# A fused two-block transformer kernel: residual and norms of the first stage by rows, modulation weights loaded in feature order, pooling branch inside the last attention steps

## The reference

```python
mod = silu(c) @ w_ada + b_ada                     # 6 x 1024
shift1, scale1, gate1, shift2, scale2, gate2 = split(mod, 6)
h = rmsnorm(x, norm_mix_g) * (1 + scale1) + shift1
proj = h @ w_in                                   # 512 pool, 3 x 512 qkv, 2 x 1024 gates
attn = attention(rope(q), rope(k), v)             # 8 heads of 64, causal
pooled = pool_mixer(proj[:, :512])                # causal window means, mixed by groups
merged = sigmoid(g_pool) * (pooled @ w_branch_pool) + sigmoid(g_attn) * (attn @ w_branch_attn)
x = x + gate1 * (merged @ w_out)
h2 = rmsnorm(x, norm_ffn_g) * (1 + scale2) + shift2
x = x + gate2 * peer_ffn(h2)                      # 8 heads x top 16 of 16384 experts per token
x = rmsnorm(x, norm_final_g)
```

## Time and profile before

| | us |
|---|---|
| median of 3 runs | 1271.32 |
| lowest, highest | 1270.78, 1272.63 |
| profiled execution | 1268.42 |
| its span, first to last instruction | 1266.6 |
| TensorE, VectorE, ScalarE busy | 1081.7, 844.0, 434.0 |
| mean granted TensorE clock | 0.947 |

### The profile page before, as it was taken

The page is one execution under the profiler, slowest core; times in us unless marked ns, Lnnn a source line. Parts: engine busy times, 40 slices in busy tenths (PEclk is TensorE's granted clock), DMA queues, the critical chain, the costliest instruction groups (busy, mean ns, idle before and its releaser), DMA issues.

```text
span 1266.6 us, 13601 instructions
## 1 busy us (share of the span) xinstructions
PE 1081.7 (85%) x5030; PEld 738.0 (58%) x5030; DVE 844.0 (67%) x1887; ACT 434.0 (34%) x879; POOL 290.7 (23%) x260
## 2 busy tenths in 40 slices
PE   1698998879899878886768778777899998999997
PEld 1697888745455334332324333322498767999986
DVE  5986774477768887878885555554664455887853
ACT  2543362232122232221322111111455444666542
POOL 0000000044344544354545435444000000000000
PEclk9798998889999989799889989899999989999999
DMA  9966643399999999999999999999773403455440
GB/s 385 404 249 266 247 185 133 133 382 398 421 396 422 421 422 421 419 413 421 421 421 421 422 421 422 421 422 421 322 291 133 150 28 122 167 200 200 177 156 33
DMA packets 47154, 389.89 MB, mean 308 GB/s; under 512 B 5361, under 2 KB 5617, under 8 KB 7154
## 3 DMA queue, kind: packets, MB, share of 16 engines
q0 software_dynamic: 36864, 268.45, 51.2%
q1 hardware_dynamic: 10226, 120.59, 24.6%
HBM read 387.97 MB, written 1.05 MB: 307 GB/s over the span
## 4 chain that ended last, share of the span: by engine, by line
PE 51%; DMA 27%; DVE 14%; ACT 4%; POOL 2%; issue 2%; SPq 0%; DVEq 0%; POOLq 0%
DMA ring<-in_uv,idx 25%; PE ps L1349 18%; PE ps L1605 14%; PE ps L1729 5%; PE ps L1371 3%; DVE ring L1153 3%; PE ps L1401 2%; POOL ring L457 2%; DVE ring_r L806 2%; PE ps L1660 2%; PE ps L1493 2%; PE ps L1511 2%; DMA ring<-in_w_ada 2%; DVE ring L817 1%; ACT ring_r L473 1%
## 5 line engine op out<-in xcount | busy, mean ns | idle before, releaser
L1605 PE MATMUL ps<-ring,probT 128*128 128x512 f32 x1024 | 493.9, 631 | 115.6 <-ACT probT L673 115.6
L1153 DVE CUSTOM_DVE_ANT_0 ring<-h2t,ring 128x1024 f32<-128x1024 f32 x256 | 309.7, 1225 | 176.0 <-DMA ring<-in_uv,idx 175.5
L457 POOL DMA_INDIRECT ring<-in_uv,idx x256 | 290.5, 1135 | 594.5 <-PE ps L1605 289.4
L1605 PEld LDWEIGHTS ps<-ring,probT 128*128 128x128 f32 x1024 | 200.7, 201 | 368.5 <-issue 209.8
L1349 PE MATMUL ps<-util_r,ring_r 128*128 128x256 f32 x1312 | 218.1, 284 | 0.4 <-DVE util_r L1125 0.4
L806 DVE TENSOR_TENSOR ring_r<-ring,ring_r 128x1024 fp32r<-128x1024 f32 x142 | 167.5, 1220 | 44.7 <-ACT ring_r L473 44.7
L1349 PEld LDWEIGHTS ps<-util_r,ring_r 128*128 128x128 f32 x1312 | 182.6, 190 | 4.7 <-issue 3.9
L473 ACT ACTIVATE ring_r<-ring 128x1024 fp32r<-128x1024 f32 x142 | 142.2, 1049 | 47.2 <-DMA ring<-in_w_in 23.7
L668 ACT ACTIVATE prob<-prob 128x4 f32<-128x4 f32 (+2 forms) x74 | 15.2, 205 | 370.4 <-DVE prob L1153 370.3
L1349 PE MATMUL ps<-h_r,ring_r 128*128 128x256 f32 x704 | 125.2, 281 | 0.6 <-DVE util_r L1125 0.6
L673 ACT ACTIVATE probT<-ct,prob 128x128 f32<-128x128 f32 x256 | 82.9, 391 | 74.9 <-DVE prob L1159 72.3
(11 more groups left out here) (210 smaller groups left out, 1005.4 us busy)
## 6 DMA issues: line engine op xcount, KB each, us to landing
ring<-in_w_in SPq DMA_DIRECT2D x13, 2048.0 KB, 10.6
ring<-in_w_ada SPq DMA_DIRECT2D x11, 2048.0 KB, 13.7
ring<-in_w_up SPq DMA_DIRECT2D x11, 2048.0 KB, 7.8
ring<-in_w_down SPq DMA_DIRECT2D x6, 2048.0 KB, 7.9
ring<-in_w_out SPq DMA_DIRECT2D x4, 2048.0 KB, 9.1
ring<-in_w_q SPq DMA_DIRECT2D x3, 2048.0 KB, 7.6
ring<-in_w_br SPq DMA_DIRECT2D x2, 2048.0 KB, 8.0
ring<-in_uv,idx POOLq DMA_INDIRECT x256, 17.5
```

Of the source, the lines that this page charges most:

```text
L457: e.indirect_dma_start(out=row_buf[n], out_offset=None, in_=uv, in_offset=bass.IndirectOffsetOnAxis(ap=idx[:, tt, k:k + 1], axis=0)).then_inc(
L1153: e.tensor_tensor_reduce(u, h2t[:, tt, :], u, 1.0, 0.0, ALU.mult, ALU.add, av[:, tt, n % 128:n % 128 + 1]).then_inc(*made.put(("dot", n)))
L1605: ins = e.matmul(acc[half][:, :], diag[:, n % 8, :], row_buf[n][:, D + half * 512:D + (half + 1) * 512], start=(k == 0), stop=(k == 127))
```

## The change

- x is loaded by rows (token on the partition). The first norm takes squares with a sum on ScalarE, a root, a reciprocal and a diagonal matrix of it on VectorE; eight products of each 128 tokens with that diagonal turn and scale x. The same again for the second norm, after an output projection by rows (512 columns a matmul, high parts of four pieces at a time) and a residual by rows with gate1 spread over the partitions. `residual_rows` is gone.
- The chunks of w_ada come in the order 0, 2, ("in", 0), 1, 3, so that shift and scale of features 0 to 511 are there first; the products with ("in", 0) are made for these features, then for the others. c comes as one row and is spread by TensorE. The constants come in two transfers.
- VectorE's list: four more low pieces stand earlier; the copies of the values go to ScalarE. Pieces 22 to 25 stand ahead of ("ada", 8).
- The four branch quarters of the pooling input are made in attention steps 7 to 10; their pieces, gatings and sigmoids in steps 5 to 10. Chunk 11 of w_ada is multiplied in step 4.

The core of the diff:

```diff
-    first = ([("ada", i) for i in range(4)] + [("in", 0)]
+    first = ([("ada", 0), ("ada", 2), ("in", 0), ("ada", 1), ("ada", 3)]
...
-    slots = [0, 1, 2, 3, 4, 0, 1, 2, 3, 1, 4, 3, 0, 2, 0, 1, 0, 3, 0, 2, 0, 2, 1, 3, 0, 2, 1, 3, 5] + [1, 0, 2, 3] * 6 + [1]
+    slots = [0, 1, 4, 2, 3, 0, 1, 2, 3, 1, 4, 3, 0, 2, 0, 1, 0, 3, 0, 2, 0, 2, 1, 3, 0, 2, 1, 3, 5] + [1, 0, 2, 3] * 6 + [1]
...
-            e.dma_start(ct[:, :], consts).then_inc(*once["ct"].put(0))
+            e.dma_start(csig[0:1, :], c_in).then_inc(*once["c"].put(0))
+            e.dma_start(ct[:, 0:CONST_FIRST], consts[:, 0:CONST_FIRST]).then_inc(*once["ct"].put(0))
             e.dma_start(cl[:, :], cols).then_inc(*once["cl"].put(0))
-            e.dma_start(crow, c_in.broadcast_to([P, D])).then_inc(*once["c"].put(0))
-            load(0)
-            load(1)
-            e.dma_start(x_sb[:, :, :].rearrange("p k t -> p (k t)"), xT).then_inc(*once["x"].put(0))
-            for n in (2, 3, 4):
+            e.dma_start(x_sb[:, :, :].rearrange("p k t -> p (k t)"), x_in).then_inc(*once["x"].put(0))
+            for n in range(5):
                 load(n)
+            e.dma_start(ct[:, CONST_FIRST:], consts[:, CONST_FIRST:]).then_inc(*once["ct2"].put(0))
...
+            act.wait_ge(once["ct"], 0)
+            sqrt_table(43)
+            for tt in range(2):
+                act.wait_ge(once["x"], 0)
+                e.activation(squared[tt], xt[:, tt, :], ACT.Square, accum_out=col(1, tt, "squares")).then_inc(
+                    *acted.put(("row squares", 1, tt, 1)))
+            for tt in range(2):
+                row_root(1, tt)
+            def modulated(k):
+                act.wait_ge(done, ("turned rows", 1, k // 2))
+                act.wait_ge(made, ("aff1", k // 4))
+                e.activation(h_sb[:, k, :], pair(("turned rows", k // 2))[:, k % 2, :], ACT.Identity,
+                             bias=mod[:, k:k + 1], scale=aff[:, k:k + 1]).then_inc(*acted.put(("modulated", k)))
+                act.wait_ge(acted, ("modulated", k))
+                e.activation(hi_r[:, k, :], h_sb[:, k, :], ACT.Copy).then_inc(*acted.put(("x high", 1, k)))
+            split_high(0)
+            modulated(0)
+            split_high(1)
+            for k in range(1, 4):
+                modulated(k)
+            split_high(2, 3)
+            for k in range(4, 8):
+                modulated(k)
             split_high(*range(4, 10))
...
+            for tt in range(2):
+                act.wait_ge(done, ("tokens", 3, tt))
+                e.activation(vt[:, tt, :], bank(("tokens", 3, tt))[:, :], ACT.Copy).then_inc(*acted.put(("v", 3, tt)))
...
+            sqrt_table(44)
+            for half in range(2):
...
+                e.activation(gate1[:, HALF[half]], bank(("gate1", half))[:, :], ACT.Copy).then_inc(
+                    *acted.put(("gate1", half)))
             for z in range(4):
                 act.wait_ge(made, ("merge", z))
                 act.wait_ge(done, ("pv", 1, 7))
                 e.activation(xm_hi[:, 2 * z:2 * z + 2, :], merged[:, 2 * z:2 * z + 2, :], ACT.Copy).then_inc(
                     *acted.put(("xm high", z)))
-            split_high(*range(44, 48))
-
-            squares(2, h_sb, made, lambda k: ("x1", k))
-            root(2, "eps")
-            shifted(2, h_sb, mod[:, 24:32])
+                split_high(44 + z)
+            def shifted(tt, k):
+                act.wait_ge(done, ("turned x1", tt, k // 4))
+                act.wait_ge(made, "aff2")
+                c = k % 4 * P
+                e.activation(h_sb[:, k, tile[tt]], bank(("turned x1", tt, k // 4))[:, c:c + P], ACT.Identity,
+                             bias=mod[:, 24 + k:25 + k], scale=aff[:, 8 + k:9 + k]).then_inc(
+                    *acted.put(("shifted", tt, k)))
+            row_squares(2, 0)
+            row_root(2, 0)
+            for k in range(KD):
+                shifted(0, k)
+            row_squares(2, 1)
+            row_root(2, 1)
+            for k in range(4):
+                shifted(1, k)
...
+            for tt in range(2):
+                row_diagonal(1, tt)
...
+            ada(0)
+            ada(2)
+            affine1(0)
+            split_low(0, 1)
+            for k in range(4):
+                x_low(1, h_sb, hi_r, k)
+            split_low(2, 3)
+            ada(1)
             ada(3)
-            split_low(0, 1)
...
-            for k in range(KD + 2):
-                if k < KD:
-                    e.tensor_scalar(h_sb[:, k, :], h_sb[:, k, :], aff[:, k:k + 1], mod[:, k:k + 1], ALU.mult,
-                                    ALU.add).then_inc(*made.put(("scaled", 1, k)))
-                if k >= 2:
-                    x_low(1, h_sb, hi_r, k - 2)
-
-            split_low(*range(2, 6))
+            affine1(1)
+            for k in range(4, 8):
+                x_low(1, h_sb, hi_r, k)
+            split_low(*range(4, 8))
             ada(4)
-            split_low(*range(6, 10))
+            split_low(*range(8, 12))
             ada(5)
-            split_low(*range(10, 14))
+            split_low(12, 13)
             rope("q")
-            split_low(14, 15)
+            split_low(*range(14, 18))
             ada(6)
-            split_low(16, 17)
+            split_low(18, 19)
             rope("k")
-            split_low(18, 19)
+            split_low(20, 21)
             ada(7)
-            split_low(*range(20, 24))
-            for tt in range(2):
-                dve.wait_ge(done, ("tokens", 3, tt))
-                e.tensor_copy(vt[:, tt, :], bank(("tokens", 3, tt))[:, :]).then_inc(*made.put(("v", 3, tt)))
+            split_low(*range(22, 26))
             ada(8)
...
+                if i == 6:
+                    four_low("xp", pT, A3r[:, 5])
+                split_low(*beside_br.get(i, ()))
+                if i >= 8:
+                    pool_gated(i - 8)
             four_low("xy", yT, A3r[:, 4])
...
+            pool_gated(3)
+            split_low(43)
...
                 dve.wait_ge(acted, ("xm high", z))
                 e.tensor_tensor(lo_r[:, 2 * z:2 * z + 2, :], m, xm_hi[:, 2 * z:2 * z + 2, :].bitcast(F32),
                                 ALU.subtract).then_inc(*made.put(("xm low", z)))
...
-
-            reciprocal(2)
-            for k in range(KD):
-                scaled(2, h_sb, x_sb, k, aff[:, 8:16])
+                if z > 0:
+                    split_low(43 + z)
+            split_low(47)
+            for tt in range(2):
+                rows_added(2, tt)
+                row_part(2, tt)
+                row_diagonal(2, tt)
+            for k in range(4, KD):
+                dve.wait_ge(done, ("turned x1", 1, 1))
+                e.tensor_scalar(h_sb[:, k, tile[1]], bank(("turned x1", 1, 1))[:, (k - 4) * P:(k - 3) * P],
+                                aff[:, 8 + k:9 + k], mod[:, 24 + k:25 + k], ALU.mult, ALU.add).then_inc(
+                    *made.put(("shifted", k)))
...
+            mixer = [group(("tokens", 0, tt)) for tt in range(2)]
+            for k0 in (0, 4):
+                for z in (0, 2):
...
+                    wait_low(q + 1)
+                    for tt in range(2):
+                        o = mixer[tt][:, z * P:(z + 2) * P].rearrange("p (q n) -> p q n", q=2)
+                        for k in range(k0, k0 + 4):
+                            pe.wait_ge(made, ("x low", 1, k))
+                            for n, (w, x3) in enumerate(((wh, hi_r), (wh, lo_r), (wl, hi_r))):
+                                ins = e.matmul(o, x3[:, k, tile[tt]], w[:, k, :, :], start=(z == 0 and k == 0 and n == 0),
+                                               stop=(z == 2 and k == 7 and n == 2))
+                        if z == 2 and k0 == 4:
+                            ins.then_inc(*done.put(("tokens", 0, tt)))
...
+                if i >= 7:
+                    branch(0, i - 7)
+            for z in range(4):
+                branch(1, z)
+                if z == 0:
+                    for half in range(2):
+                        o = group(("gate1", half))
+                        pe.wait_ge(made, "mod2")
...
+            for tt in range(2):
+                for half in range(2):
+                    o = group(("mix1", tt, half))[:, :]
+                    o4 = o.rearrange("p (q n) -> p q n", q=4)
...
+                    wait_low(QUARTER["out", half, 3])
+                    for k in range(KD):
+                        pe.wait_ge(made, ("xm low", k // 2))
+                        for n, (to, w, x3) in enumerate(((o4, wh, xm_hi), (o4, wh, lo_r), (o, wl, xm_hi))):
+                            ins = e.matmul(to, x3[:, k, tile[tt]], w[:, k], start=(k == 0 and n == 0),
+                                           stop=(k == KD - 1 and n == 2))
+                    ins.then_inc(*done.put(("mix1", tt, half)))
+                    banks.give(("mix1", tt, half), made, ("gated rows", 2, tt, half))
+            for tt in range(2):
+                turned_x1(tt)
```

429 lines of the change are left out of this document (207 added, 222 removed).

## The result

The changed kernel takes 1277.24 us, median of 8 runs (1274.10 to 1280.83), beside 1271.68 for the kernel before in the same comparison (8 runs). The ratio is 1.0043, with a 95% interval of 1.0028 to 1.0058: slower by 0.43%. The forecast was 1271.0 with a range up to 1276.0, so both the forecast and its range were missed. Its profiled execution took 1275.14, with a span of 1273.3; the one before took 1268.42, with 1266.6.

What follows compares the result with a forecast made beforehand. DMA-bound gathers (262 to 899 us) stay fixed, so only the first query matmul shifts: output projection 224.0 plus norm 6.8 gives 230.8 against 231.2, -0.4, hence 1271 us; range 1265.5 to 1276.

Steps and rivals of the forecast that it cites:

- VectorE's stand for ("in", 6): Before the attention: ("in", 6), queued behind chunk 8, lands 13.1 after its pair's issue; VectorE's lead of 5 is gone.
- Start, chunk 7, VectorE's stand: Up to the first mask: first projections done 49.2, chunk 7 done 94.4, VectorE stands from 97, first mask 115.5.
- Second wait to head 4: TensorE waits about 128 to 131; ScalarE's probabilities copy ends 140.7, then 2.2 to head 4's scores at 142.9.
- Steps 7 to 10: Four pooling-branch quarters between attention head steps, 2.9 each; TensorE ends these at 183.8.
- Attention branch: Four quarters after a wait of some 3 for the attention's low parts; with gate1, 1.7, they end at 200.1.
- Merge: VectorE's merge steps with a piece each, 3.9, follow the branch quarters; last low piece ready at 206.9.
- The norm: Output projection to queries: 6.8, including second squares 1.4, root, reciprocal and diagonal 0.9, four small matmuls 0.9, shift 0.4.
- Rival (d): Merge and norm by rows slower, by handovers or 512-column matmuls: +3, 1274.3; chance 0.08.
- (a): Transfers without a tail: both pairs land 11.7 after issue, chain 2.8 shorter, 1268.2; chance 0.20.
- (b): VectorE does not stand at ("in", 6); attention begins 5 to 9 earlier, 7 reaches the end, 1264.3; chance 0.13.
- (c): Lower clock behind TensorE's waits at 110 and 128, counted as nothing in the forecast: +4.5, 1275.8; chance 0.17.
- The late arrival is made up here: Output projection ends at 224.0 against 224.3, as half of its work starts before the merge ends.

Runs made afterwards that it cites:

- run 1: Changed kernel with chunk 8 multiplied on VectorE ahead of low pieces 24 and 25, not behind them: 1267.01 us, ratio to the kernel before 0.9968.
- run 2: Changed kernel with SyncE issuing ("in", 6) ahead of chunk 8 and ("in", 7) ahead of chunk 9: 1264.49 us, ratio to the kernel before 0.9950.
- run 3: Changed kernel with SyncE's order of run 2 and VectorE's chunks 8 to 11 in attention steps 0, 2, 4 and 5: 1261.17 us, ratio 0.9920.
- run 10: Kernel before, not the changed one, with the SyncE and VectorE orders of run 3: 1269.3 us beside 1269.66, ratio 1.0003.
- run 5: Changed kernel with the pooling branch's four quarters and their pieces, gatings and sigmoids put back behind the attention: 1276.92 us, ratio to the kernel before 1.0057.
- run 7: Changed kernel with gate1 behind the last branch quarter and VectorE's low pieces 44 to 47 behind the merge steps: 1274.5 us, ratio 1.0031.
- run 6: Changed kernel with the attention result's high and low parts made ahead of weight pieces 41 and 42 and the third gating: 1274.19 us, ratio 1.0040.
- run 4: Changed kernel with tile 1's squares ahead of most of tile 0's shifts on ScalarE, behind the output projection: 1271.79 us, ratio 1.0015.
- run 12: Changed kernel with 88 and 30 extra matmuls filling TensorE's waits at the first pool mixing and in the norm; both waits overrun: ratio 1.0229.
- run 8: Changed kernel with the edits of run 3, run 4, run 6 and run 7 together: 1250.89 us, ratio to the kernel before 0.9853.
- run 9: Kernel of run 8 with each low part of the merge made one step later on VectorE: 1247.4 us, ratio to the kernel before 0.9823.

## Why the prediction was wrong

The mechanism that it put first, VectorE's stand for ("in", 6) and what hangs on it, was right. The sum behind it was too low by 7.2 us at the first query matmul (238.0 for 230.8), and its own steps divide that (the table above, differences between one milestone and the next). Two steps failed. The prediction "counted nothing" for the lower clock behind TensorE's waits, and 4.7 of the 7.2 are that: 1.0 and 0.6 at head 4, 1.5 at the attention branch, 1.6 in the norm. And it priced the end of the norm at "four small matmuls 0.9, one shift 0.4", where TensorE makes eight.

- **Start, chunk 7, VectorE's stand: right**, within 1 us in every milestone up to the first mask. VectorE stood 11.4 where it had "from 97 until 107.6 + 1.0". The reason is shown by runs 1 to 3: either order shortens the stand (to 6.8 and 2.9), and 8 to 16 us go with it. Run 10 shows the other half, that the kernel before had no such lead to lose. TensorE's own wait was wrong in place and length: it stood 11.0, from 108.1, at the first pool mixing, whose window copy ScalarE makes behind the exponentials of the first mask and two high pieces, and not 5.6 for a PSUM bank. That cost nothing, as the next wait was shorter for it, 1.0 for 3.
- **Second wait to head 4: +0.9.** ScalarE's copy of the turned probabilities ended at 140.6, as predicted (140.7). From there the term "2.2 more to the scores of head 4" took 3.1, at a clock of 0.62. Runs 5 and 7 have 2.1 at full clock.
- **Steps 7 to 10: +1.8.** A quarter takes 3.11, not 2.9, which is 0.8 for four; 0.6 is head 4's scores at the lower clock; the rest was not followed.
- **Attention branch: +1.3.** The wait of 3 was right (2.7), but the quarter behind it took 4.6 for 3.1, at a clock of 0.61. Run 6 has neither.
- **Merge: +0.4, output units: 17.1 as predicted.** That a 512-column matmul costs two of 256 was right.
- **The norm: +2.8**, 9.6 for 6.8. The largest single miss. The prediction had written down the mechanism, shifts ahead of squares on ScalarE, and priced the way to the diagonal nearly right (6.0 to the second turn, for 5.5). What failed is the step "four small matmuls 0.9, one shift 0.4": TensorE makes eight before a query matmul can start, behind a wait of 4.2 and so at the lower clock, 3.6. At full clock they take 2.0 (run 4), so 0.7 of the miss is their number and 1.6 the clock. Rival (d) had this place and size (+3) at a chance of 0.08, which was too little for a chain of which no row had shown the length.

Of the rivals, (a) fell (the pairs took 12.5 and 13.5, not 11.7), and (b) fell. (c) was right in that the clock falls behind the waits, and its reason for counting nothing held for the first loss: the 2.5 behind the wait of 11.0 fell into slack. It had not looked at the shorter waits behind, where the 4.7 came. They were not among the bounds from which the range's upper end of 1276 was made. Rivals (b), (c) and (d) were also priced from 1271.3, the median before, and not from the sum's 1270.9, which changes nothing here.

"The late arrival is made up here", in the output projection, was right in its form: the attention's 6.0 (143.8 for 137.8) and the branches' 10.6 became 4.1 at the end of the output projection (228.4 for 224.3). Then the norm by rows took 2.7 more than the norm by features (9.6 for 6.9).

What stays open: how the clock's share falls on a given execution. In runs 4 and 7 the same code between head 4's scores and the branches was 2.0 longer or 0.6 shorter than in the changed kernel. Nor was the norm by rows tried alone, without the rest of the change.

## What to carry to other kernels

When a change gives one engine a lead, look for the first transfer that this engine's partner needs, and for what stands ahead of it in the transfer queue: here two free slots waited 7 and 15 us behind another load, and reordering the queue turned a loss of 0.4% into a gain of 0.5%, with VectorE's list in step 0.8%. A lead is worth having only if the engine that bounds behind it is the one that gained it; the same reordering was worth nothing on the kernel whose TensorE was already full. Price a serial tail over three engines by its queue order and at the lower clock, and give TensorE's work behind every wait of the lengths seen here (1.9 to 11.0) that clock as the upper bound.

## What the runs showed of the hardware

- Of two 2 MB transfers issued 0.4 apart the second landed 12.5 and 13.5 after the first issue, while the first of such a pair was there after 7.7 (run 1, issued at 95.12, multiplied from 102.86). Issued 6.6 apart, they took 8.7 and 7.5, each from its own issue (run 2).
- The same wait of 2.7 at the attention branch was followed by a quarter of 4.59 at a clock of 0.61 in the changed kernel, of 3.07 in run 2, and of 3.08 at 1.00 in run 12, whose row in the table of stretches is:

```profile
210.90:214.00 3.10, 3.07 (x26) 3.10 (x27) 2.62 (x5) 1.18 (x2) 0.00 (x0) 1.00 0.51 209
```

Waits of 1.5 cost no clock in runs 4, 8 and 9; one of 1.9 in run 8 did. The wait of 2.0 at the values of head 0 was followed by a clock of 0.62 in the changed kernel and of 1.00 in runs 5 and 7. So a wait of 1.9 to 2.7 prices the work behind it only as a range.
- A float32 matmul of 256 columns took 0.43 and of 128 columns 0.23 (run 12: 88 in 38.15, 30 in 6.86), beside 0.12 for 256 columns of the fast passes.
